# RWKV-7 chunk inverses in 32x32 products instead of 64x64 products, one kernel of a hybrid diffusion trunk

## The reference

```
def step(s, inp):
    r_t, w_t, k_t, v_t, kk_t, a_t = inp
    sa = jnp.einsum('bhvk,bhk->bhv', s, kk_t)
    s = (s * w_t[:, :, None, :] - sa[..., None] * (kk_t * a_t)[:, :, None, :]
         + v_t[..., None] * k_t[:, :, None, :])
    y = jnp.einsum('bhvk,bhk->bhv', s, r_t)
    return s, y
```

## Time and profile before

| what | us |
|---|---|
| median of three runs | 2048.72 |
| the three runs | 2044.47, 2048.72, 2058.74 |
| the profiled execution, own time | 2042.87 |
| its span in the trace | 2040.6 |
| TensorE busy (PE) | 1923.5 |
| TensorE weight loads (PEld) | 1732.5 |
| VectorE busy | 1038.2 |
| ScalarE busy | 712.0 |

### The profile page before, as it was taken

One profiled execution on the slowest core, in us unless ns is written; L12 is line 12 of the kernel. 1 busy time (PEld: TensorE's weight loads), 2 busy tenths in 40 slices (PEclk: granted clock), 3 DMA queues, 4 the chain that ended last, 5 costly groups with the idle time before them and its releaser, 6 DMA issues.

```text
span 2040.6 us, 37381 instructions
## 1 busy us (share of the span) xinstructions
PE 1923.5 (94%) x16214; PEld 1732.5 (85%) x16214; DVE 1038.2 (51%) x1623; ACT 712.0 (35%) x1192; POOL 34.4 (2%) x69
## 2 busy tenths in 40 slices
PE   6999999998889899999999999999988889999996
PEld 5899997986669769999989999989766787899996
DVE  2333335655566685333364333466446748633336
ACT  3222223445532343222252222245463324422221
POOL 0000000000000001000000000000000000000000
PEclk8999999999989999999999999999988799999998
DMA  7733336333661045333344333323244003433320
GB/s 323 294 123 125 127 129 238 113 115 124 247 279 70 26 165 182 129 124 123 124 165 145 123 123 123 127 81 124 104 166 178 3 4 122 170 124 123 123 103 31
DMA packets 41472, 277.71 MB, mean 136 GB/s; under 512 B 4778, under 2 KB 6810, under 8 KB 9344
## 3 DMA queue, kind: packets, MB, share of 16 engines
q1 hardware_dynamic: 35424, 255.34, 34.6%
q0 software_dynamic: 3312, 16.91, 2.1%
q10 hardware_dynamic: 2608, 3.56, 0.5%
HBM read 269.22 MB, written 3.41 MB: 134 GB/s over the span
## 4 chain that ended last, share of the span: by engine, by line
PE 82%; DVE 11%; ACT 3%; issue 2%; DMA 1%; ACTq 0%; SPq 0%; POOL 0%; DVEq 0%; POOLq 0%
PE bank L981 17%; PE bank L916 17%; PE bank L920 16%; PE bank L919 16%; PE bank L756 3%; PE bank L1369 1%; PE bank L1358 1%; PE bank L1376 1%; DVE ring_r L2158 1%; PE bank L765 1%; DVE ln_stat L2177 1%; DVE x L2175 1%; PE bank L837 1%; DVE arena L2168 1%; DMA ring<-weights 1%
## 5 line engine op out<-in xcount | busy, mean ns | idle before, releaser
L2158 DVE TENSOR_TENSOR ring_r<-ring,arena_r 128x1024 fp32r<-128x1024 f32 x328 | 387.8, 1222 | 703.7 <-ACT arena_r L1647 703.1
L916 PE MATMUL bank<-arena_r 128*128 128x384 f32 (+3 forms) x2056 | 698.7, 340 | 13.1 <-DVE arena_r L2207 10.8
L920 PE MATMUL bank<-arena_r,ring_r 128*128 128x384 f32 (+2 forms) x1816 | 603.3, 332 | 0.0
L919 PE MATMUL bank<-arena_r 128*128 128x384 f32 (+2 forms) x1816 | 601.5, 331 | 0.0
L916 PEld LDWEIGHTS bank<-arena_r 128*128 128x128 f32 x2056 | 389.9, 190 | 35.6 <-issue 19.4
L1647 ACT ACTIVATE arena_r<-ring 128x1024 fp32r<-128x1024 f32 x340 | 340.3, 1052 | 137.8 <-PE bank L920 136.6
L919 PEld LDWEIGHTS bank<-arena_r 128*128 128x128 f32 x1816 | 342.2, 188 | 3.5
L920 PEld LDWEIGHTS bank<-arena_r,ring_r 128*128 128x128 f32 x1816 | 342.2, 188 | 0.0
L981 PE MATMUL bank<-arena_r 128*128 128x512 f32 x1128 | 310.9, 393 | 0.3 <-issue 0.3
L1778 ACT ACTIVATE arena<-bank 128x384 f32<-128x384 f32 x88 | 43.3, 492 | 736.1 <-PE bank L920 736.1
L981 PEld LDWEIGHTS bank<-arena_r 128*128 128x128 f32 x1128 | 210.7, 188 | 42.2 <-issue 1.2
(11 more groups left out here) (293 smaller groups left out, 1834.9 us busy)
## 6 DMA issues: line engine op xcount, KB each, us to landing
ring<-weights SPq DMA_DIRECT2D x242, 1024.0 KB, 4.9
lnrow<-ln_in POOLq DMA_DIRECT2D x6, 1024.0 KB, 5.9
const<-consts POOLq DMA_DIRECT2D x1, 2211.0 KB, 9.5
arena<-gate POOLq DMA_DIRECT2D x4, 385.0 KB, 8.0
x<-x_in ACTq DMA_DIRECT2D x1, 1536.0 KB, 13.7
rows<-row_in POOLq DMA_DIRECT2D x2, 704.0 KB, 10.4
par<-par_in POOLq DMA_DIRECT2D x2, 662.5 KB, 7.6
y_out<-x SPq DMA_DIRECT2D x2, 512.0 KB, 2.6
```

The costliest lines, as they stand in the source:

```text
L916: mm = pe.matmul(out, w_h, h_h, start=start, stop=False, skip_group_check=True)
L919: pe.matmul(out, w_h, h_l, start=False, stop=False, skip_group_check=True)
L920: return pe.matmul(out, w_l, h_h, start=False, stop=stop, skip_group_check=True)
L2158: ve.tensor_tensor(low_unit((l, name), u) if out is None else out, raw, place.bitcast(F32), ALU.subtract).then_inc(w_ready, 1)
```

## The change

TensorE computes only what the masks keep, or near to it. A new function `level_products` issues the products of one group, level and kind (`lx` for L1358, `xlx0` for L1369, `xlx1` for L1376). For w up to 16 each 64x64 product becomes two 32x32 products, one for each half e of the chunk, and of the 32 columns only the 16 that the mask keeps are moved; `side` picks them (every other run of w columns). They land in their own places of the same bank. For w = 32 each product becomes one 32x32 product, from the half of the chunk where the factor is not zero to the half that is kept. Banks, copies, masks, semaphores and the order of the kinds stay as they are.

```diff
+                        def side(t, w, upper):
+
+                            return t.rearrange("p (n s w) -> p n s w", s=2, w=w)[:, :, upper, :]
+
+                        def level_products(v, g, bank, kind):
+
+                            w = 1 << v
+                            for d in range(2):
+                                for h, _, _, c in heads_chunks():
+                                    o = 64 * (4 * d + h)
+                                    x0, x1, low = xz[:, 0, g, d, h, :], xz[:, 1, g, d, h, :], am[:, g, d, h, :]
+                                    got, to = wsb[:, g, o:o + 64], ps[bank][:, o:o + 64]
+                                    if w == 32:
+                                        far = slice(64 * c + 32 * (1 - d), 64 * c + 32 * (1 - d) + 32)
+                                        near = slice(64 * c + 32 * d, 64 * c + 32 * d + 32)
+                                        rows, cols = slice(32 * d, 32 * d + 32), slice(32 * (1 - d), 32 * (1 - d) + 32)
+                                        if kind == "lx":
+                                            mm = pe.matmul(to[near, cols], low[far, rows], x0[far, cols], start=True, stop=True)
+                                        else:
+                                            mm = pe.matmul(to[near, cols], x1[near, rows], got[near, cols], start=True, stop=True)
+                                        continue
+                                    for e in range(2):
+                                        k, m = slice(64 * c + 32 * e, 64 * c + 32 * e + 32), slice(32 * e, 32 * e + 32)
+                                        if kind == "lx":
+                                            mm = pe.matmul(side(to[k, m], w, 1 - d), low[k, m], side(x0[k, m], w, 1 - d),
+                                                           start=True, stop=True)
+                                        elif kind == "xlx0":
+                                            mm = pe.matmul(side(to[k, m], w, 1 - d), x1[k, m], side(got[k, m], w, 1 - d),
+                                                           start=True, stop=True)
+                                        else:
+                                            mm = pe.matmul(side(to[k, m], w, d), got[k, m], side(x1[k, m], w, d),
+                                                           start=True, stop=True)
+                            return mm
...
-                                for d in range(2):
-                                    for h, _, _, c in heads_chunks():
-                                        k, o = slice(64 * c, 64 * c + 64), 64 * (4 * d + h)
-                                        mm = pe.matmul(ps[LX_BANK[g]][k, o:o + 64], am[k, g, d, h, :], xz[k, 0, g, d, h, :],
-                                                       start=True, stop=True)
-                                mm.then_inc(lx_mm, 1)
+                                level_products(v, g, LX_BANK[g], "lx").then_inc(lx_mm, 1)
...
+                                level_products(v, g, XLX_BANK[g], "xlx0").then_inc(xlx0_mm, 1)
...
+                                    level_products(v, g, LX_BANK[g], "xlx1").then_inc(xlx1_mm, 1)
```

More of the change, by code:

```diff
@@ L1365, in rwkv_units @@
                                     pe.wait_ge(xz_ready, g + 1)
[L1366 to L1371, removed]
-                                if v < RW_LEVELS - 1:
[L1373 to L1378, removed]
+                                level_products(v, g, XLX_BANK[g], "xlx0").then_inc(xlx0_mm, 1)
+                                if v < RW_LEVELS - 1:
+                                    level_products(v, g, LX_BANK[g], "xlx1").then_inc(xlx1_mm, 1)
                         def by_token(bank, src, g, done):
```

## The result

The changed kernel takes **2112.5 us** (median of four runs, 2111.3 to 2114.4) against 2051.1 for the kernel before in the same session (2044.5 to 2058.7). The ratio is 1.031, 95% interval 1.027 to 1.034. The forecast was 2018 us, faster; its range ended at 2042. The profiled execution of the changed kernel spans 2111.1 us, 70.5 more than that of before, which was one of the fastest runs of its kernel; the difference of the medians is 61.

The account below looks back on a forecast made before the run. TensorE was taken to bound the inversion. Savings of 3.0 (level 1), 8.9 (levels 2 to 4) and 2.35 us (level 5) made 14.3 a layer, 28.5 for two: 2014 or 2020 us, forecast 2018, range 2004 to 2042.

Parts of the forecast that it names:

- the issue price: TensorE in inversion levels 1 to 4: records issued every 9.1 ns, so a group of 64 takes 0.58 us.
- Rival (c): Inversion's instructions cannot be supplied: some 19 packets a layer; gain gone at 2.07 us a packet, 2043 us, slower beyond; 5%.
- The loop through VectorE's copies: From one inversion level to the next, through the third group and VectorE's six copies: 5.43 us a level against 8.40.
- Level 5: Last inversion level, 16 products of 32x32 a group at 0.47 us: 2.35 us saved a layer.
- Tile pace: TensorE in the inversion: the wider side sets a tile's pace, 29.2 ns a record for 32 stationary columns, half of 58.3.
- Rival (a): Inversion levels 1 to 4: four row tiles take turns at their PSUM bank, 14.6 ns a record; 2038 to 2044 us; 9%.
- Rival (b): TensorE's granted clock falls to half, 1.2 GHz, in or behind the inversion: 2026 to 2032 or 2043 to 2053 us; 9%.
- Rival (d): Inversion products: fixed start cost of 29.2 ns a record, however narrow; a group 1.87 us, total 2110 us, slower; 5%.

Follow-up runs that it names:

- the loop: Changed kernel with levels 1 to 4 as a hardware loop of four passes on TensorE, 32x32 products with all 32 columns; 2049.7 us, ratio 1.000 to the kernel before.
- kept-columns kernel: Kernel before with levels 1 to 4 in 64-row products on only the 32 kept columns, level 5 in 32x32 products; 2080.7 us, ratio 1.017.
- the old products as a loop: Kernel before with its 64x64 products of levels 1 to 4 in a hardware loop, level 5 in 32x32 products; 2052.6 us, ratio 1.001.

## Why the prediction was wrong

**The step that failed is the issue price.** "Issue: 48 records of 32x32 on eight tiles last 0.62 us", 9.1 ns each, was carried over to 2496 pairs a layer. As the pace inside a block it was right: 127 records last 1.33 us, less the 0.18 of the last one, 9.2 ns from start to start. But 48 records are less than one block of 128, so that row could not show what the 129th waits for. With 3.6 us a block a pair costs 28 ns, a group of 64 costs 1.8 us instead of 0.58, a level 4.5 blocks or 16.2 us instead of 5.43.

**Rival (c) was the right mechanism with the wrong price.** It counted the packets well (19 a layer) and named its sign, idle time called issue, which is what the trace shows. It took the packet's own 0.94 us for the cost of a packet (from a rounded share; the trace of before has 1.07 on average) and priced the case at 2043, where the gain is just gone, at 2.07 us a packet; beyond that it said slower, and gave no time. The chance was 5%. With 3.6 us its own sum gives 19.5 x 3.6 = 70 us for a stage of 39.9, some 60 us more for two layers, which is what happened.

The price stood in the trace of before, unread. The stage after the inversion consists of short products too, and the chain there has these pieces (start us, length us, what):

```profile
681.05 0.48 issue
...
683.98 1.13 issue
...
688.23 0.34 issue
...
691.29 0.83 issue
```

TensorE goes on at 681.53, 685.11, 688.57 and 692.12: 3.58, 3.46 and 3.55 us apart, with 127, 128 and 128 pairs between, and the clock there is not in doubt:

```profile
678.00:693.00 15.00, 12.21 (x580) 11.72 (x572) 5.44 (x15) 3.18 (x8) 0.00 (x0) 1.00 0.02 4
```

The same period at a clock of 1.00 as at 0.50 in the changed kernel: the supply does not follow TensorE's clock. In the inversion itself the pieces of the earlier trace rows give 29.2 ns a pair, 3.73 us for 128, with hardly a stop (0.26 us at 626.09, after 127 pairs): it stood just above that period, so that pairs added there had to show. In all these stretches DMA moved no more than 5 GB/s on average; what a block costs beside weight transfers no run shows.

The Trainium skill (Runtime: NRT & Kernel Launch, Instruction fetch mechanics) says that instructions come in 16 KiB blocks of 256, that the next one is fetched while the current one runs, and that the cost of a block is mostly hidden. The first agrees with the trace (18 packets for 4608 instructions more), and so does the second, in that a packet starts 1.0 to 1.6 us after TensorE has gone on; the last does not hold where 128 pairs run in 1.3 us.

**What is late next: not VectorE.** The loop through VectorE's copies, 5.43 us a level, was to bound the levels. In the changed kernel VectorE waits for TensorE instead, about 2 us at a time (2.25 and 1.98 us before its copies at 637.40 and 640.96). Where the supply was out of the way the term was near: passes of 6.0 and 5.6 us at full clock in the first layer of the loop. In its second layer the chain does go through VectorE's six copies, from 1644.67 to 1648.45, one each 0.61 us; 0.64 was forecast.

**Level 5: near, as work.** 2.35 us a layer were forecast; with level 5 alone changed, the stage became shorter by 1.4 and 2.1 us, with stops of 1.13 and 0.79 us in it at the floor of its blocks.

**Tile pace: right in kind.** The wider side sets it (first layer of the kept-columns kernel), and 29.2 ns was the products' pace (the old products as a loop). Half of 58.3 for 32 columns was a little too dear: where level 5 alone was changed, its first two groups started 0.38 us apart in both layers, at full clock, and not 0.47.

**Rival (a)**, four row tiles that take turns of 14.6 ns at a bank: no. The 64 records of a group go from four row tiles into one bank, and 127 records started 9.2 ns apart. The rule of the Trainium skill that was cited for it (TensorEngine Tiling (Array Packing), Gotcha 1: PSUM Pressure), that row tiles cannot access one bank at once, cost nothing that these runs show; whether the tiles take shorter turns they do not tell. **Rival (b)**, the clock: it did fall, at 627.7, after a stretch of 3.6 us in which TensorE was busy for 2.0, and came back just before 700; but in the inversion it cost nothing that can be seen: the 128 pairs of a burst start within 1.7 us instead of 1.2, inside a period that stayed. Behind the inversion it held up the next products (54 records in the 3.9 us from 696.1, at a clock of 0.58, where before 82 ran in the 4.0 us from 664.0 at 1.00): from the last load of the inversion to the first L1530 it is 30.9 us in each layer, against 29.0 and 29.4 to that line's old number L1511, 3.3 us in all. **Rival (d)**, a start cost for every pair, forecast 2110, and 2112 came. That is chance: it took the products' 29.2 ns for the cost, and the supply's 28 lies beside it. The bursts at 9.2 ns a pair refute it. The Trainium skill's 25 ns as the least from start to start (TensorE: Matmul & The Clock Gate, Wait — 56ns, not 53.3ns?) does not hold from tile to tile in them either; on each of the four tiles it is some 37 ns.

What stays open: what the 3.6 us consist of beyond the packet (1.0 to 1.6 us ahead of it, 1.2 to 1.6 behind it). That TensorE goes on at so even a distance after each packet suggests that it waits for this packet, but whether a packet holds the next block or the one after the trace does not say.

## What to carry to other kernels

Before splitting products on TensorE, count the instructions that the stage executes as straight code, in blocks of 256, and hold them against the distance of stops called issue in a stretch of short products of the same kernel; a queue's share of busy time says nothing of a price that consists of delays. A short run of instructions, under one block, shows the pace of issue and not that of supply. The hardware loop here, of 1152 instructions a pass, paid the supply in its first pass only; the straight code before, with more work in each instruction (29.2 ns a pair against 28), paid next to nothing.

## What had not been expected of the hardware

- A block of 256 TensorE instructions was to be had each 3.3 to 4.1 us, 3.5 to 3.7 on average over a layer, at a granted clock of 1.00 and of 0.50 alike, with the packet itself taking about 1 us of it.
- Loop passes of 1152 instructions ran without new packets: in the loop's second to fourth pass, 19 us, one packet was moved, and TensorE stopped only 0.1 to 0.5 us between passes.
- With half of the columns moving in 64-row products, TensorE busy throughout, the clock was 1.00 in one layer and 0.50 in the other, 38.3 against 63.7 us.
